# One row factor for two chained norms, and the first two projection tiles interleaved

## The reference, cut to what matters

```python
def rmsnorm(x, g):
    y = x * lax.rsqrt(jnp.mean(x * x, axis=-1, keepdims=True) + EPS)
    return y * g
# end of the first block (x is its residual sum)
x = rmsnorm(x, final_g)
# start of the second block
mod = silu(c) @ w_ada + b_ada                  # shift, scale, gate
h = rmsnorm(x, norm_g_2) * (1.0 + scale) + shift
proj = h @ w_in_2                              # 8 heads of q, k, v, z; then the recurrent half
q, k = rmsnorm(q, q_g), rmsnorm(k, k_g)        # over the 128 numbers of a head
# softmax(q k^T + bias) v, gated by silu(z), and so on
x = x + gate * (y @ w_out_2)                   # needs the first norm's result again
```

## Time and profile before

| | us |
|---|---|
| median of three runs | 2023.4 |
| the three runs | 2023.3, 2023.4, 2025.51 |
| profiled execution, its own time | 2024.33 |
| its span | 2022.5 |
| PE busy | 1951.1 (96%) |
| DVE busy | 1098.7 (54%) |
| ACT busy | 790.7 (39%) |
| POOL busy | 263.4 (13%) |

### The profile page before, as it was taken

How to read it: one execution, slowest core, us unless ns; L and a number is a source line. 1 busy time by engine, 2 the same in 40 slices (tenths; PEclk the granted TensorE clock), 3 DMA queues, 4 the chain that set the end, 5 groups by cost and what they waited for, 6 DMA issues and landing times.

```text
span 2022.5 us, 25791 instructions
## 1 busy us (share of the span) xinstructions
PE 1951.1 (96%) x9018; PEld 1586.5 (78%) x9018; DVE 1098.7 (54%) x1456; ACT 790.7 (39%) x1086; POOL 263.4 (13%) x210
## 2 busy tenths in 40 slices
PE   5899999999999999998899999999999999998999
PEld 4788787778888876886688888887888888886887
DVE  6634457777777747766644444444554555555332
ACT  4433333333333363322534334444555555554111
POOL 4500000000000001433200000000323333221000
PEclk8899999999999999999899999999999999998999
DMA  6322324444444425675122222222211222122442
GB/s 241 125 104 83 146 104 143 175 164 170 172 165 169 168 78 176 231 248 185 70 86 86 82 80 82 82 83 81 84 63 73 72 83 83 62 83 94 145 145 73
DMA packets 49535, 244.63 MB, mean 121 GB/s; under 512 B 5592, under 2 KB 6872, under 8 KB 28640
## 3 DMA queue, kind: packets, MB, share of 16 engines
q1 hardware_dynamic: 49056, 241.05, 33.7%
q10 hardware_dynamic: 448, 3.17, 0.4%
HBM read 235.79 MB, written 8.41 MB: 121 GB/s over the span
## 4 chain that ended last, share of the span: by engine, by line
PE 89%; DVE 5%; ACT 3%; issue 2%; POOL 1%; DMA 0%; DVEq 0%; SPq 0%; ACTq 0%; POOLq 0%
PE ps_p L523 26%; PE ps_p L525 26%; PE ps_p L524 26%; PE ps_s L734 2%; PE ps_o L602 2%; PE ps_s L582 2%; DVE w_lo L1166 1%; PE ps_t L592 1%; ACT w_hi L799 1%; PE ps_x L540 1%; DVE hd L1593 1%; DVE hA L1615 0%; DVE act_lo L1508 0%; PE ps_x L565 0%; PE ps_o L759 0%
## 5 line engine op out<-in xcount | busy, mean ns | idle before, releaser
L523 PE MATMUL ps_p<-act_hi,w_hi 128*128 128x512 f32 x2384 | 964.5, 405 | 28.5 <-DVE act_lo L1508 8.7
L525 PE MATMUL ps_p<-act_hi,w_lo 128*128 128x512 f32 x2384 | 935.6, 392 | 0.0
L524 PE MATMUL ps_p<-act_lo,w_hi 128*128 128x512 f32 x2384 | 933.7, 392 | 0.0
L523 PEld LDWEIGHTS ps_p<-act_hi,w_hi 128*128 128x128 f32 x2384 | 451.5, 189 | 132.1 <-issue 33.2
L525 PEld LDWEIGHTS ps_p<-act_hi,w_lo 128*128 128x128 f32 x2384 | 450.7, 189 | 98.2
L524 PEld LDWEIGHTS ps_p<-act_lo,w_hi 128*128 128x128 f32 x2384 | 452.0, 190 | 86.2 <-issue 1.4
L799 ACT ACTIVATE w_hi<-raw 128x2048 fp32r<-128x2048 f32 x157 | 299.9, 1911 | 425.8 <-PE ps_p L525 413.1
L1166 DVE TENSOR_TENSOR w_lo<-raw,w_hi 128x2048 fp32r<-128x2048 f32 x157 | 361.3, 2301 | 159.5 <-ACT w_hi L799 149.4
L1362 DVE CUSTOM_DVE_ANT_0 mkv<-mkv,c_all 128x1024 f32<-128x1024 f32 x96 | 146.2, 1559 | 0.2 <-DVE hcol L1481 0.2
L1699 POOL TENSOR_TENSOR ssq_a<-ssq_a,wk 128x512 f32<-128x512 f32 x15 | 35.9, 2395 | 774.9 <-ACT wk L1028 774.9
L1171 DVE SCALAR_TENSOR_TENSOR wk<-ps_p,wk 128x512 f32<-128x512 f32 x44 | 30.4, 692 | 173.1 <-ACT wk L816 173.0
(11 more groups left out here) (226 smaller groups left out, 1643.6 us busy)
## 6 DMA issues: line engine op xcount, KB each, us to landing
raw<-wt_dram SPq DMA_DIRECT2D x157, 1024.0 KB, 4.8
mkv<-ada_dram SPq DMA_DIRECT2D x96, 512.0 KB, 4.6
Y<-xT_dram SPq DMA_DIRECT2D x4, 1024.0 KB, 10.6
qkv<-xT_dram SPq DMA_DIRECT2D x16, 256.0 KB, 2.8
spill_dram<-Y SPq DMA_DIRECT2D x16, 256.0 KB, 2.2
hqk<-spill_dram SPq DMA_DIRECT2D x16, 256.0 KB, 2.7
out_dram<-wk SPq DMA_DIRECT2D x16, 256.0 KB, 2.0
Y<-memT_dram SPq DMA_DIRECT2D x4, 512.0 KB, 7.9
```

Of the source, the lines that this page charges most:

```text
L523: mm(o, wh, hi[:, k, 0:n], start=at == 0, stop=False)
L524: mm(o, wh, lo[:, k, 0:n], start=False, stop=False)
L525: last = mm(o, wl, hi[:, k, 0:n], start=False, stop=at == KT - 1)
```

## The change

Four things are changed. **One factor.** r1·r2 is computed from a single sum. With m the mean of x² and mg the mean of (g·x)², r1·r2 = 1/sqrt(mg + EPS·m + EPS²), which is the mean of x²·(g²+EPS) under the root. `c_act`, free by then, is filled with sqrt(g²+EPS) ahead of `out1` and is the scale of the second square; the scaled square now comes ahead of the plain one. At the seam ACT makes the factor straight from `ps_o`. r1 itself, which `out2` needs, is made by ACT from `ps_x` ahead of the third of the 16 tiles. **The key's weights.** DVE alone splits them (`split_whole`), before it waits for the factor. **The first pair.** In head 0 PE issues query and key step by step in turn up to step 9 (`LEAD`), then the query's steps 10 to 15, then the key's. **Head 0 by itself.** It is written out ahead of the loop; in it ACT copies the query out of PSUM, both row sums stand in the value tile (behind steps 1 and 6), and three of the score products one step later (11, 12, 15). In the heads 1 to 7 nothing moves.

```diff
+            def first_pair():
+                pe.wait_ge(w_split, tile_no("att", 0, 1) + 2)
+                for j in range(2):
+                    pe.wait_ge(evac[slot("att", j)], half("att", 0, j) + 1)
+                steps = [(j, k) for k in range(LEAD) for j in range(2)]
+                steps += [(j, k) for j in range(2) for k in range(LEAD, KT)]
+                for j, k in steps:
+                    s = slot("att", j)
+                    if j == 0:
+                        pe.wait_ge(h_odd, k // 2 + 1) if k % 2 else pe.wait_ge(moving, 1 + 2 * KT + k // 2 + 1)
...
-                project("att", i, 0, use="h")
-                project("att", i, 1, hooks={4: lambda: side("att", i, 0, sum_rows(...))})
-                project("att", i, 2, hooks={4: lambda: side("att", i, 1, sum_rows(...)),
-                                            10: lambda: scores("att", i, 0, q, k, chunk_b),
+                if isinstance(i, int):
+                    first_pair()
+                    sums, scored = {1: lambda: square_sum(0), 6: lambda: square_sum(1)}, (11, 12, 15)
...
-            rows(r1[:, :], ps_x[:, :], D, wk[:, 2, :]).then_inc(norm2_rows.sem, 1)
-            act.wait_ge(norm2_mean.sem, norm2_mean.at("norm2", 0, 1))
-            rows(wk[:, 2, :], wk[:, 3, :], D, wk[:, 2, :]).then_inc(norm2_rows.sem, 1)
+            act.wait_ge(norm2_sum, 1)
+            o.step(fn(wk[:, 2, :], ps_o[:, :], ACT.Ln, scale=1.0 / D, bias=col("eps_square")))
+            o.settle()
+            fn(wk[:, 2, :], wk[:, 2, :], ACT.Exp, scale=-0.5).then_inc(norm2_rows.sem, 1)
             for k in range(KT):
+                if k == 2:
+                    act.wait_ge(side_full.sem, side_full.at("norm2", 0, 1))
+                    o.step(fn(r1[:, :], ps_x[:, :], ACT.Ln, scale=1.0 / D, bias=eps_c))
+                    o.settle()
+                    act.sem_inc(side_free.sem, 1)
+                    o.step(fn(r1[:, :], r1[:, :], ACT.Exp, scale=-0.5))
...
+                    if isinstance(i, int) and j == 0:
+                        src = qkv2[:, 0, :]
+                        o.step(fn(src, ps_p[:, slot("att", j), :], ACT.Copy))
+                        o.settle()
+                        act.sem_inc(evac[slot("att", j)], 1)
...
+            split_whole("att", 0, 0)
             dve.wait_ge(norm2_rows.sem, norm2_rows.at("norm2", 0, 1))
-            do(tt(wk[:, 3, :], ps_o[:, :], r1[:, :], ALU.mult))
-            dve.sem_inc(side_free.sem, 1)
-            tt(wk[:, 3, :], wk[:, 3, :], r1[:, :], ALU.mult).then_inc(norm2_mean.sem, 1)
-            dve.wait_ge(norm2_rows.sem, norm2_rows.at("norm2", 0, 2))
-            do(tt(wk[:, 2, :], wk[:, 2, :], r1[:, :], ALU.mult))
```

More of the change, by code:

```diff
@@ L694, in both_sums @@
                 mm(ps_x[:, :], ones, ssq_a[:, :], start=True, stop=False)
+                pe.wait_ge(squares_ready.sem, squares_ready.at("out1", 7, 3))
+                mm(ps_o[:, :], ones, wk[:, 3, :], start=False, stop=True).then_inc(norm2_sum, 1)
                 pe.wait_ge(squares_ready.sem, squares_ready.at("out1", 7, 4))
-                mm(ps_o[:, :], ones, wk[:, 3, :], start=False, stop=True)
                 return mm(ps_x[:, :], ones, wk[:, 1, :], start=False, stop=True)
             side("norm2", 0, 0, both_sums)
+            LEAD = 10
@@ new lines, in first_pair @@
+            def first_pair():
[8 more added lines that the diff above has]
+                        pe.wait_ge(h_odd, k // 2 + 1) if k % 2 else pe.wait_ge(moving, 1 + 2 * KT + k // 2 + 1)
+                    wh, wl = w_hi[:, s, k * P:(k + 1) * P], w_lo[:, s, k * P:(k + 1) * P]
+                    mm(ps_p[:, s, :], wh, act_hi[:, k, :], start=k == 0, stop=False)
+                    mm(ps_p[:, s, :], wh, act_lo[:, k, :], start=False, stop=False)
+                    last = mm(ps_p[:, s, :], wl, act_hi[:, k, :], start=False, stop=k == KT - 1)
+                    if k == KT - 1:
+                        last.then_inc(proj_done, 1)
@@ L714, in att @@
                 weigh("att", i, 3, qkv2[:, 3, :], tp2[:, 1, :])
-            loop(pe, "att", att)
+            loop(pe, "att", att, head=1)
             def hg(i):
@@ L1036, in out1 @@
                 squares(i, 0)
+            act.wait_ge(gain_square, 1)
+            o.step(fn(c_act[:, :], c_act[:, :], ACT.Ln, bias=eps_c))
+            o.settle()
+            o.step(fn(c_act[:, :], c_act[:, :], ACT.Exp, scale=0.5))
             loop(act, "out1", out1, head=1, order=o)
@@ L1059, in norm @@
                         act.wait_ge(heads_done.sem, heads_done.at("att", i, 0))
-                    o.step(fn(wk[:, 0, :], ps_p[:, slot("att", j), :], ACT.Square))
+                    src = ps_p[:, slot("att", j), :]
+                    if isinstance(i, int) and j == 0:
+                        src = qkv2[:, 0, :]
+                        o.step(fn(src, ps_p[:, slot("att", j), :], ACT.Copy))
+                        o.settle()
+                        act.sem_inc(evac[slot("att", j)], 1)
+                    o.step(fn(wk[:, 0, :], src, ACT.Square))
                     o.settle()
@@ L1069, in norm_rows @@
                     fn(wk[:, 1, :], wk[:, 1, :], ACT.Exp, scale=-0.5).then_inc(rms_rows.sem, 1)
-                split("att", i, 0)
-                norm(0)
-                split("att", i, 1)
+                if isinstance(i, int):
+                    split("att", i, 1)
+                    norm(0)
+                else:
+                    split("att", i, 0)
+                    norm(0)
+                    split("att", i, 1)
                 norm_rows(0)
@@ L1086, in att @@
                 gate_exp("att", i, 3, dst=2)
-            loop(act, "att", att, order=o)
+            loop(act, "att", att, head=1, order=o)
             def hg(i):
@@ L1164, in split, with split_whole @@
                 s = (TILE0[phase] + j + ahead) % 2
+                dve.wait_ge(w_hi_done, t + 2)
+                tt(w_lo[:, s, :], raw[:, s, :], w_hi[:, s, :].bitcast(F32), ALU.subtract).then_inc(w_split, 1)
+            def split_whole(phase, i, j, ahead=1):
+                t = tile_no(phase, i, j) + ahead
+                s = (TILE0[phase] + j + ahead) % 2
+                dve.wait_ge(s_raw[s], 16 * (half(phase, i, j + ahead) + 1))
+                dve.wait_ge(proj_done, t)
+                dve.tensor_copy(w_hi[:, s, :], raw[:, s, :]).then_inc(w_hi_done, 1)
                 dve.wait_ge(w_hi_done, t + 2)
@@ L1563, in att @@
                 tt(Y[:, i, :], ps_o[:, :], wk[:, 3, :], ALU.mult).then_inc(heads_done.sem, 1)
-            loop(dve, "att", att, order=o)
+            loop(dve, "att", att, head=1, order=o)
             o.settle()
@@ L1794 @@
     put("eps", EPS)
+    put("eps_square", EPS * EPS)
     n = np.arange(P)
```

46 lines of the change are left out of this document (31 added, 15 removed).

## The result

| | before | changed |
|---|---|---|
| median, us | 2024.1 | 2009.05 |
| profiled execution | 2024.33 | 2008.55 |
| its span | 2022.5 | 2006.8 |

The ratio of the changed kernel's runs to those before is 0.9925, with a 95% interval of 0.9908 to 0.9942. The forecast was 2013.1, with a range of 2010.8 to 2017.0: the direction was right, and the gain was 15 us instead of 10.

The account below looks back on a forecast made before the run. The prediction took PE as the bound, starved at the seam of the two blocks. 11.5 us gained less 1.26 given back made 10.3, so 2014.0 against the profiled execution and 2013.1 against the median, range 2010.8 to 2017.0.

Parts of the forecast that it names:

- What bounds the kernel: PE, busy 1951.1 of 2022.5 us; the seam has about 12 us without PE work, then some 13 us of starving.
- The factor: At the seam, scaled square first: factor ready at 955.55, which alone would let the first scaled tile start 5.1 us earlier.
- The split of the key's weights: On DVE ahead of the tiles: copy 1.23 us (slow end 2.29), first scaled tile at 956.85, 3.84 earlier.
- The sixteen tiles: Chain of DVE, ACT and POOL: 25.16 us plus 0.6 for r1's pair on ACT, last low part at 982.6.
- The pair: Query and key steps interleaved on PE in head 0: last query matmul at 983.8, between 983.2 and 984.5.
- The gate that is late next: Value's weights, split after the query's end: value tile starts at 988.7 instead of 1000.23, 11.5 us gained.
- What is given back: Losses in head 0 from row sums, the key's factor and later score products: 1.26 us, bounds 0.46 and 2.
- the cost of nothing for the written-out head: Head 0 written out ahead of the loop: more code, the same work, so its cost was set at nothing.
- A: Rival: PE's clock stays low through the pair; 2019.8 us in mild form (chance 0.08), 2024.6 in full (0.03).
- B: Rival: at the seam the factor counts and the pair doesn't; gain 3.8 less 1.26, 2020.9 us, chance 0.04.
- C: Rival: DVE and POOL slow each other in the sixteen tiles, period 10.6 instead of 6.24, 2031 us, chance 0.02.
- the three terms of the low end: Range's low end, 2010.8: 0.6 for full clock at the end, 0.6 for free r1 pair, 0.8 for waits that don't come.

Follow-up runs that it names:

- x3_factor: Kernel before plus only the combined factor, scaled square first and r1 ahead of the third tile, no pair or early split: 2016.06 us.
- z1: Kernel before plus one unused DVE fill ahead of `out1`, timed again beside the kernel before: 2019.28 us, ratio 0.997.
- z2: The changed kernel itself, timed again beside the kernel before on the same chip: 2009.68 us, ratio 0.9923.
- x2_peel: Kernel before with only head 0 of the second attention written out ahead of the loop on PE, ACT and DVE: 2019.61 us.
- y1: Kernel before plus one unused DVE fill of a single column ahead of `out1`: 2018.21 us.
- y2: Kernel before plus the same unused DVE fill, placed behind the recurrent heads: 2024.84 us.
- v3: Kernel before plus one unused single-column copy on ACT, with the wait for its end, ahead of `out1`: 2024.92 us.
- x1: Kernel before with one unused column more at the end of the small constants' tile: 2023.27 us.
- y3: Changed kernel plus an unused DVE fill right ahead of the fifth subtraction of each recurrent head: 2013.3 us, heads of 55.9 us.
- y4: Changed kernel with the high part of the key's weights copied by POOL, DVE only subtracting: 2008.69 us.
- z4: Changed kernel with POOL copying the high part of the key's weights, timed again beside the kernel before: 2009.42 us, ratio 0.9921.
- x4_pair: Changed kernel without the combined factor; interleaved pair, early split, written-out head and unused column stay: 2012.57 us.
- z3: Changed kernel with POOL's copy of the key's weights, plus twelve unused products ahead of query steps 11, 12, 13 and 15: 2010.11 us, ratio 0.9926.
- v1: Kernel before plus four unused DVE fills ahead of `out1`: 2021.48 us, recurrent heads of 55.2 us.
- v2: Kernel before plus sixteen unused DVE fills ahead of `out1`: 2018.52 us, recurrent heads of 55.2 us.

## Why the prediction was wrong

By its own steps, in its order:

- *What bounds the kernel.* Right for the seam. "Behind it PE has no hole that this change touches" is half of the step that failed. PE's wait of 3.8 us in the recurrent heads stands in the list of PE's waits over the whole program before, and the prediction neither priced it nor named it: its rows of waits end at 1010 us.
- *The factor.* 955.55 forecast, 955.58 measured. x3_factor shows the 5.1 us by itself.
- *The split of the key's weights.* The copy took 1.23, the value taken, and the slow end is out. The tile started at 957.26 instead of 956.85, by the 0.6 that DVE came later to its copy, less 0.2 that I had put between the steps.
- *The sixteen tiles.* From the first scaled tile to the last low part 25.30 instead of 25.76. The pair for r1 cost 0.14, not 0.6. The last low part is at 982.56, forecast 982.6.
- *The pair.* The clock rose earlier than assumed at the start (0.94 from 963 to 971), and fell again at the end (0.66 from 981). The query's last matmul starts 0.51 ahead of ACT's copy, near 984.35, where I had taken 983.8 between 983.2 and 984.5. The end for the fallen clock was the right one.
- *The gate that is late next.* Right: the value tile waits for `w_lo`, 0.28 us, and starts at 989.16, forecast 988.7.
- *What is given back.* 11.07 at the value tile less 9.65 at the probabilities: 1.4, forecast 1.26. The waits came as said at the second row sum (0.30) and the first turned probabilities (0.21).
- *The sum.* The seam's 10.3 measured 9.65, and 9.6 in the timed comparison of z1 and z2. With it alone the time would have been 2014.5 (2024.1-9.6), inside the range. Against the profiled execution the forecast was 2014.0 and 2008.55 came, 5.5 less: 5.3 from the recurrent heads and 1.0 from `out2`, less 0.8 that the seam and `out1` fell short.
- *The step that failed* is "From there on all starts are about 10.3 us earlier, to the end", with the cost of nothing for the written-out head, "more code, the same work". The recurrent heads went from 55.9 to 55.2 us, 5.3 in all. In its place the runs show that all eight edits of DVE's program ahead of these heads turned a contest in them. The written-out head alone does this (x2_peel), the factor alone too (x3_factor), one unused DVE instruction ahead of them too (y1), one behind them (y2), one on ACT (v3) and a moved column (x1) don't. The mechanism is shown by y3: a tenth of a microsecond decides whether DVE or POOL goes first. That it turned in this direction was luck, and no part of the change's merit.
- *The clock at the start of `out2`* gave the last 1.0 us. From the last recurrent head on, the first eight us ran at 0.51 before and at 0.65 after (the earlier trace rows have the columns; the stretches are 1840 to 1848, and 1825.2 to 1833.2). I had not counted it. Two profiles of one kernel agree to 0.3 us in the length of this phase (181.4 and 181.7 changed, 181.7 twice with the fill ahead), but it varies by 1.0 from kernel to kernel, and with the clock at its start: 182.3 to 182.4 us at 0.51 to 0.53 (before, y4, z4), 181.4 to 181.7 at 0.61 to 0.65 (changed, z2, y1, z1). Why a kernel falls to one side is not shown.

Of the rivals, A (the clock stays low) is out by the clock of 0.94 and 1.00 from 963 to 977, and B (the pair doesn't count) by x4_pair, which gains 6.0 alone. C named the right resource, the meeting of DVE and POOL, at the wrong place and with the wrong sign. Its price was also too high: the slowed pair of scaled tiles costs 2.43-1.42 = 1.0 more and not 1.1, and all six operations would add 3.8 and not 4.4 us a period, so 2028 and not 2031. And the three terms of the low end (0.6, 0.6, 0.8) lead from 2013.1 to 2011.1 and not to 2010.8. Neither slip touches the forecast.

**What stays open.** In the kernel before the difference starts 0.1 to 0.4 us later behind DVE's copy than in the changed one, and all kernels in which DVE's instructions ahead of the recurrent phase are those of before share it (x1, y2, v3), while none of the eight edits that alter them has it (x2, x3, x4, y1, y4, z3, v1, v2). That makes the place of DVE's instructions in the program the cause that fits, but no row shows how the place delays a start, and with which period it would come back: one, four and sixteen more all had the short head. It could be that the place makes the difference late and so it loses, or asks in time and loses by less than the records tell; y3 shows only that being late is enough.

## What to carry to other kernels

An edit's own gain and the gain of whatever it shifts are different numbers. Compare the two traces phase by phase, up to phases that the edit doesn't touch, and run the kernel before with an idle instruction ahead: if that alone moves the time, its gain is no merit of the edit. Before a forecast, list the main engine's small waits over the whole program, and where one repeats once a round because two engines that slow each other start within 0.1 us, count it as a coin that any edit may turn. To order such instructions by a dependency instead of leaving it to the race is the natural next step; no run here tried it.

## What the hardware showed that I had not expected

- A contest of DVE and POOL, with starts within 0.1 us of each other: the outcome was the same in all eight rounds of every profile, and in both profiles of each of the three kernels that have two, and it turned with one unused instruction some 600 us earlier. Price 0.7 us a round.
- DVE's copy of 128x2048 from fp32 into fp32r took 1.23 us, POOL's 1.89 and ACT's 1.9, and while POOL copied, a DVE addition of two columns took 0.88 instead of 0.16.
- PE's clock at the end of the same thin stretch of matmuls was 0.57 in one kernel and 1.00 in another that differs by 0.6 us in when its tiles come.
